# Two successive norms as one factor at the seam of two blocks, with X normed beside the next projection

## The chip, the cores and the metric

The kernel runs on one NeuronCore of a Trainium2 chip. The metric is the device time of one execution in microseconds. Engines are named as in the profile: PE is TensorE (matmuls), PEld its weight loads, DVE is VectorE, ACT is ScalarE, POOL is GpSimd, SP issues the weight DMAs.

## The reference

A token matrix X (256 tokens of 1024 features) passes through a first block of two layers, a final norm, and a second block of two layers. The parts at the seam:

```python
def _rmsnorm(x, g):
    x32 = x.astype(jnp.float32)
    y = x32 * lax.rsqrt(jnp.mean(x32 * x32, axis=-1, keepdims=True) + EPS)
    return (y * g.astype(jnp.float32)).astype(x.dtype)
...
    # the end of a layer of first_block
        gate = jax.nn.sigmoid((_rmsnorm(x, g[3]) @ ple_w_gate[li]).astype(jnp.float32))
        x = x + (gate * (p[li] @ ple_w_in[li]).astype(jnp.float32)).astype(x.dtype)
...
    return _rmsnorm(x, final_norm)
...
def second_block(x, c, w_ada, b_ada, g_pre, g_post, w_in, w_out, pe_k, pe_v, w_ck1, w_ck2, w_cv1, w_cv2):
    cs = jax.nn.silu(c)
    for l in range(DEPTH):
        mod = cs @ w_ada[l] + b_ada[l]
        shift, scale, gate = mod[:, None, :D], mod[:, None, D:2 * D], mod[:, None, 2 * D:]
        h = rmsnorm(x, g_pre[l]) * (1.0 + scale) + shift
        y = hybrid_mixer(h, w_in[l], w_out[l], pe_k[l], pe_v[l], w_ck1[l], w_ck2[l], w_cv1[l], w_cv2[l])
        x = x + gate * rmsnorm(y, g_post[l])
```

`hybrid_mixer` begins with `u = h @ w_in`. So the final norm of the first block is followed at once by the first norm of the second block. With r1 the first norm's factor of a token and G the final gain, the second factor is 1/sqrt(mean((x r1 G)^2) + EPS).

## The kernel before, in words

X lies in SBUF transposed: 128 partitions by 8 tiles (k) of 256 tokens; a "pair" m or j is two tiles, 512 columns. A sum over features is a matmul of `ones` with squares (`sums_pair`), which leaves the sum of each token in every partition of a PSUM bank.

Each engine runs its own program, written out by hand; engines wait for each other by semaphore counts (`when(name)` is the count at which the step `name` is done, `did(...)` counts a step). An engine works strictly in the order of its program, so whatever stands behind a waiting instruction waits too.

All weights stream through one ring of chunks of 1 MB. SP loads a chunk into one of two buffers `w_raw`, in two halves. `hi(c)` on ACT rounds it to `w_hi`, `lo(c)` on DVE makes the rest `w_lo`; both have four slots. A load of chunk c waits for `lo(c - 2)`, a `hi(c)` for PE's end of chunk c - 4. PE multiplies each chunk in three passes (`three`), which is 48 matmuls of 256 columns for a group of 256 output features. In the names below `ple1` has five chunks (c to c + 4) and the next, c + 5, is `win0`, the first of the 16 of the second block's projection; `AHEAD` is 3.

The work around the change, in program order:

- `ple(1, 9, 7, 7)`: the gate of layer 1. PE makes four groups into banks 4 to 7 (`pgate`). For each group j, DVE multiplies it by the norm factor `rs` into `pg`, ACT takes the sigmoid, and DVE's `finish(j)` multiplies by `pp` and adds to X. ACT squares each finished pair (`last_squares`): once plain into `sq`, and once with the final gain as scale into `sq_f`.
- PE sums both sets pair by pair, `sums_pair(8, m)` and `sums_pair(9, m, sq_f)`. Ahead of the last pair stands `mod_sums(3, 1)`: 24 one-column matmuls that sum the second block's modulation over partitions, into bank 1; `modulation` on DVE adds the bias into `mods`.
- The final norm: `root(8)` (Sqrt on ACT) and `inv(8)` (reciprocal on DVE) give r1. DVE multiplies the weighted sums by r1 squared (`mean_f`), ACT takes the Sqrt of that. POOL has multiplied X by G, and POOL and DVE multiply it by r1, two pairs each.
- The norm of layer l = 0 of the second block: `inv(9)`, then for each tile `scaled(k)` on DVE, `xh` on ACT (rounded, with the shift added) and `xl` on DVE (the rest).
- The projection, 16 groups of `WIN` (`qm`, `qm`, `km`, `km`, `vm`, ...) into banks 0 to 7 in turn. The first group takes the tiles as they come; DVE or ACT copies each group out (`proj`). While PE is on group n, ACT and DVE make `hi` and `lo` of chunk `win0` + n + 3.
- Ahead of its copies DVE builds the tables `bias` and `cbias`. X itself is next read at the end of the layer, where the mixer's output is added.

Of the kernel before, what the change touches and what calls it, by code (L numbers as in the profile page):

```python
# [24 lines left out]
P = 128  # L25
# [89 lines left out]
def chunk_table():  # L115
# [11 lines left out]
    return first, n  # L127


def build(nc, io, known):  # L130
# [396 lines left out]
    def _(pool):  # L527
        did = Steps(at)
        nc.gpsimd.memset(ones[:, :], 1.0).then_inc(*did(pool_steps))
        nc.gpsimd.memset(eps[:, :], EPS).then_inc(*did(pool_steps, "memsets"))  # L530
# [111 lines left out]
        for m in range(4):  # L642
            pool.wait_ge(*when(("sq", 9, m)))
            gain = col0[:, 95 + 2 * m:97 + 2 * m].unsqueeze(2).to_broadcast([P, 2, T])
            G.tensor_tensor(X[:, 2 * m:2 * m + 2, :], X[:, 2 * m:2 * m + 2, :], gain, ALU.mult).then_inc(*did(pool_steps, ("x_gain", m)))
        pool.wait_ge(*when(("rs", 8)))
        for m in (2, 3):
            pool.wait_ge(*when(("x_gain", m)))
            G.tensor_tensor(X[:, 2 * m:2 * m + 2, :], X[:, 2 * m:2 * m + 2, :], rep(rs[:, :], 2), ALU.mult).then_inc(*did(pool_steps, ("x", 9, m)))
        pool.wait_ge(*when(("sums", 9)))  # L650
        for l in range(2):

            pool.wait_ge(*when(("x", 9 + l, 3)))
# [3 lines left out]

            for kv, name in enumerate(("ck", "cv")):
# [10 lines left out]
    def _(act):  # L669
# [192 lines left out]
        def ple(l, nu, v, s):  # L862
            c = first[f"ple{l}"]
            norm(nu, v, g_norm(l, 3), s, ("chunk", first[f"out{2 * l + 1}"] - 1), [c - 1 + AHEAD, c + AHEAD])
            for j in range(4):
                if j in (0, 2):
                    hi(c + 1 + j + AHEAD)
                if j == 0:
                    hi(c + 2 + AHEAD)
                    root(s)  # L870
                if l == 0 and j >= 1:
                    high(5, 4, g_kv, j - 1, xh2)
                if l == 1 and j >= 1:
                    last_squares(j - 1)
                act.wait_ge(*when(("pg", l, j)))
                A(pg[:, 2 * j:2 * j + 2, :], pg[:, 2 * j:2 * j + 2, :], ACT.Sigmoid).then_inc(*did(act_steps, ("pgs", l, j)))
            if l == 0:
                high(5, 4, g_kv, 3, xh2)
            else:
                last_squares(3)  # L880
            hi(c + 4 + AHEAD)

        def last_squares(m):
# [3 lines left out]
            A(sq[:, pair_, :], X[:, pair_, :], ACT.Square).then_inc(*did(act_steps, ("sq", 8, m)))  # L887
            for k in (2 * m, 2 * m + 1):
                A(sq_f[:, k, :], X[:, k, :], ACT.Square, scale=g_final(k)).then_inc(*did(act_steps, ("sq", 9, m)))
# [98 lines left out]
        root(8)  # L988
        act.wait_ge(*when("mean_f"))
        A(std[:, :], std[:, :], ACT.Sqrt, bias=eps[:, :], scale=1.0 / D).then_inc(*did(act_steps, ("std", 9)))  # L990

        for l in range(2):
# [8 lines left out]
            c0 = first[f"win{l}"]  # L1001
# [1476 lines left out]
```

## Time and profile before

| what | value |
|---|---|
| device time, median of 3 runs | 1559.37 us (1559.15 to 1560.65) |
| the profiled execution: its time | 1557.95 us |
| the profiled execution: its span | 1556.1 us |
| mean granted clock of TensorE | 0.979 of full |
| PE busy | 1491.3 us, 96% of the span |
| DVE, ACT, POOL busy | 70%, 49%, 12% |

The span runs from the first to the last instruction of one profiled execution, and all times of rows are microseconds from its start. "Idle before <-releaser" tells how long an engine stood before an instruction and whose step it waited for. A granted clock of 1.00 is 2.4 GHz, 0.50 is 1.2 GHz.

### The profile page before, as it was taken

Reading aid. Unit: us, or ns where it says so; the run is one execution under the profiler, and the core shown is the slowest. Engines: PE = TensorE matmul, PEld = TensorE weight load, DVE = VectorE, ACT = ScalarE, POOL = GpSimd, SP = SyncE. Lnnn points to the kernel's source line nnn. Section 1 sums busy time; section 2 is a strip of 40 time slices with the busy share of each in tenths; the row PEclk is TensorE's granted clock in tenths of the full one; section 3 lists DMA queues with packets and bytes.
Section 4 is the critical chain, followed back from the end, with each engine's and each line's share of the span. In section 5 each row is a group of like instructions: output and inputs, shape, how many; then the busy total and the mean of one; then the engine's idle time right before and its main releaser. Section 6 shows DMA issues by size and latency. Waiting matters only on the chain.

```text
span 1556.1 us, 31034 instructions
## 1 busy us (share of the span) xinstructions
PE 1491.3 (96%) x12371; PEld 1436.0 (92%) x12371; DVE 1095.1 (70%) x1566; ACT 766.3 (49%) x1149; POOL 189.7 (12%) x227
## 2 busy tenths in 40 slices
PE   6999998999999999999999999999996999989998
PEld 6999998999999998999999899999996996879867
DVE  5886568986896677876677755887568557395683
ACT  5554355465554356444454454544354436354472
POOL 1111013711331010101010001110012000010000
PEclk9999999999999999999999999999997998999999
DMA  7787743345787646766646135776653751066400
GB/s 226 230 271 231 246 147 124 90 128 162 236 271 229 211 136 191 246 219 215 217 129 177 55 122 173 233 251 218 223 160 108 208 149 55 1 181 186 125 1 28
DMA packets 219308, 264.86 MB, mean 170 GB/s; under 512 B 22253, under 2 KB 197325, under 8 KB 219213
## 3 DMA queue, kind: packets, MB, share of 16 engines
q1 hardware_dynamic: 209136, 234.58, 48.5%
q0 software_dynamic: 8960, 27.37, 5.3%
q10 hardware_dynamic: 1117, 1.57, 0.3%
q8 instruction: 68, 1.11, 0.3%
q14 instruction: 27, 0.22, 0.1%
HBM read 262.44 MB, written 1.05 MB: 169 GB/s over the span
## 4 chain that ended last, share of the span: by engine, by line
PE 81%; DVE 12%; ACT 4%; DMA 2%; issue 1%; POOL 0%; SPq 0%; DVEq 0%; ACTq 0%
PE twin L1081 24%; PE twin L1082 24%; PE twin L1083 24%; DVE w_lo L1774 3%; DMA w_raw<-in_ffn_w_in 1%; PE twin L1488 1%; PE twin L1700 1%; ACT w_hi L700 1%; DVE rs L1803 1%; DVE hg_s L1992 1%; PE twin L1502 1%; PE twin L1500 1%; PE twin L1662 1%; DVE hg_f L1974 1%; DVE sq L1973 1%
## 5 line engine op out<-in xcount | busy, mean ns | idle before, releaser
L700 ACT ACTIVATE w_hi<-w_raw 128x1024 fp32r<-128x1024 f32 (+1 forms) x452 | 453.6, 1038 | 459.3 <-PE twin L1083 279.9
L1081 PE MATMUL twin<-xh,w_lo 128*128 128x256 f32 x2312 | 653.5, 283 | 26.2 <-DVE xl L2260 15.0
L1774 DVE TENSOR_TENSOR w_lo<-w_raw,w_hi 128x1024 fp32r<-128x1024 f32 (+1 forms) x452 | 548.1, 1249 | 166.0 <-ACT w_hi L700 165.6
L1082 PE MATMUL twin<-xl,w_hi 128*128 128x256 f32 x2312 | 648.4, 280 | 0.0
L1083 PE MATMUL twin<-xh,w_hi 128*128 128x256 f32 x2312 | 648.2, 280 | 0.0
L1081 PEld LDWEIGHTS twin<-xh,w_lo 128*128 128x128 f32 x2312 | 440.3, 190 | 31.4 <-DVE xl L2260 16.1
L1082 PEld LDWEIGHTS twin<-xl,w_hi 128*128 128x128 f32 x2312 | 439.6, 190 | 1.5 <-issue 1.2
L1083 PEld LDWEIGHTS twin<-xh,w_hi 128*128 128x128 f32 x2312 | 438.1, 189 | 0.2
L1081 PE MATMUL twin<-hh,w_lo 128*128 (+1 forms) x704 | 195.6, 278 | 0.0
L1082 PE MATMUL twin<-hl,w_hi 128*128 (+1 forms) x704 | 195.2, 277 | 0.0
L1083 PE MATMUL twin<-hh,w_hi 128*128 (+1 forms) x704 | 195.2, 277 | 0.0
L543 POOL DMA_DIRECT2D mod_raw<-in_w_ada x128 | 68.9, 542 | 527.4 <-DVE mod_acc L1823 401.2
L1081 PEld LDWEIGHTS twin<-hh,w_lo 128*128 128x128 f32 x704 | 132.9, 189 | 0.0
L1082 PEld LDWEIGHTS twin<-hl,w_hi 128*128 128x128 f32 x704 | 132.2, 188 | 0.0
L1083 PEld LDWEIGHTS twin<-hh,w_hi 128*128 128x128 f32 x704 | 132.1, 188 | 0.0
L1823 DVE SCALAR_TENSOR_TENSOR mod_acc<-mod_raw,csf,mod_acc 128x384 f32<-128x384 f32 x112 | 65.2, 617 | 39.7 <-DMA mod_raw<-in_w_ada 39.4
L622 POOL TENSOR_TENSOR sq<-sq 128x1024 f32<-128x1024 f32 x7 | 16.9, 2408 | 394.3 <-ACT sq L722 394.3
L706 ACT ACTIVATE xh<-X,col 128x256 fp32r<-128x256 f32 x72 | 32.0, 500 | 49.8 <-DVE X L1797 27.8
L665 POOL TENSOR_TENSOR y<-y,rs 128x512 f32<-128x512 f32 x4 | 6.9, 1738 | 343.5 <-DVE rs L1803 343.5
L1850 DVE TENSOR_TENSOR gate_t<-twin,rs 128x512 f32<-128x512 f32 x44 | 30.2, 687 | 26.1 <-PE twin L1083 26.0
L1858 DVE TENSOR_TENSOR up_t<-twin,rs 128x512 f32<-128x512 f32 x44 | 30.2, 686 | 23.6 <-PE twin L1083 23.6
L1081 PE MATMUL twin<-w_hi,xl 128*128 128x256 f32 x160 | 45.5, 285 | 0.0
(363 smaller groups left out, 2077.4 us busy)
## 6 DMA issues: line engine op xcount, KB each, us to landing
w_raw<-in_ffn_w_in SPq DMA_DIRECT2D x176, 512.0 KB, 4.7
w_raw<-in_ffn_w_out SPq DMA_DIRECT2D x88, 512.0 KB, 4.2
w_raw<-in_w_in SPq DMA_DIRECT2D x52, 512.0 KB, 4.7
mod_raw<-in_w_ada POOLq DMA_DIRECT2D x128, 192.0 KB, 4.4
w_raw<-in_a_w_in SPq DMA_DIRECT2D x32, 512.0 KB, 4.2
w_raw<-in_ple_w_gate SPq DMA_DIRECT2D x16, 512.0 KB, 4.2
w_raw<-in_b_w_out SPq DMA_DIRECT2D x16, 512.0 KB, 3.7
w_raw<-in_w_out SPq DMA_DIRECT2D x16, 512.0 KB, 4.5
```

Of the source, the lines that this page charges most:

```text
L543: pool.dma_start(mod_raw[:, n % 2, :], io["w_ada_2"][l][P * k:P * (k + 1), col:col + MOD_COLS]).then_inc(sem[f"mod_landed{n % 2}"], 16)
L622: G.tensor_tensor(sq[:, 0:4, :], sq[:, 0:4, :], sq[:, 4:8, :], ALU.add).then_inc(*did(pool_steps))
L700: A(w_hi[:, c % NSLOT, cols], w_raw[:, c % NRAW, cols], ACT.Copy).then_inc(*did(hi_ready))
L706: A(xh[:, k, :], X[:, k, :], ACT.Copy, scale=gain(k)).then_inc(*did(act_steps, ("xh", nu, k)))
L1081: mm(out, lhs[1], rhs[0], start=start, stop=False, skip_group_check=skip)
L1082: mm(out, lhs[0], rhs[1], start=False, stop=False, skip_group_check=skip)
L1083: return mm(out, lhs[0], rhs[0], start=False, stop=stop, skip_group_check=skip)
L1488: last = nc.tensor.transpose(bank[4 + h][:, dst * P:(dst + 1) * P], p[:, h, src * P:(src + 1) * P], ident)
L1774: V.tensor_tensor(w_lo[:, c % NSLOT, cols], w_raw[:, c % NRAW, cols], f32(w_hi[:, c % NSLOT, cols]), ALU.subtract).then_inc(*did(lo_ready))
L1823: V.scalar_tensor_tensor(acc, raw, cs, acc, ALU.mult, ALU.add).then_inc(sem["mod_steps"], 1)
L1850: V.tensor_tensor(gate_t[:, p % 2, :, :], two(bank[b][:, :]), rep(rs[:, :], 2), ALU.mult).then_inc(*did(gate_scaled))
L1858: V.tensor_tensor(up_t[:, p % 2, :, :], two(bank[b + 1][:, :]), rep(rs[:, :], 2), ALU.mult).then_inc(*did(up_scaled))
```

## The change

The final norm and the next norm become one factor. Since r1 = 1/sqrt(mean(x^2) + EPS), the product of both factors is 1/sqrt(mean((G^2 + EPS) x^2) + EPS^2). So one sum of squares, weighted by the root of G^2 + EPS (`gain_r`, computed once from the gains), gives the factor that takes X to the normed input of the projection; G itself goes into `gpre`. The plain squares are still summed, after the weighted ones; their factor (`std` 9 in the old tile `cos`, its reciprocal in `sin`) is made during the projection and applied to X there, one tile in each of the turns 4 to 11. POOL no longer multiplies X. In `ple(1)` DVE takes the products of groups 0 and 1 before `finish(0)` and so on, ACT takes each sigmoid before the squares of the pair before, and a Sqrt of one column stands before the last squares. `mod_sums(3, 1)` moves behind the third group of the projection, its `modulation` to DVE's fourth turn; POOL's loads of the compression weights (`wc`) wait for it. Two `lo` move behind `finish(3)` and behind the `xl`.

```diff
@@ POOL
-        for m in range(4):
-            pool.wait_ge(*when(("sq", 9, m)))
-            gain = col0[:, 95 + 2 * m:97 + 2 * m].unsqueeze(2).to_broadcast([P, 2, T])
-            G.tensor_tensor(X[:, 2 * m:2 * m + 2, :], X[:, 2 * m:2 * m + 2, :], gain, ALU.mult).then_inc(*did(pool_steps, ("x_gain", m)))
-        pool.wait_ge(*when(("rs", 8)))
-        for m in (2, 3):
-            pool.wait_ge(*when(("x_gain", m)))
-            G.tensor_tensor(X[:, 2 * m:2 * m + 2, :], X[:, 2 * m:2 * m + 2, :], rep(rs[:, :], 2), ALU.mult).then_inc(*did(pool_steps, ("x", 9, m)))
         pool.wait_ge(*when(("sums", 9)))
         for l in range(2):
-            pool.wait_ge(*when(("x", 9 + l, 3)))
+            pool.wait_ge(*when(("x", 8 + 2 * l, 3)))
...
+            pool.wait_ge(*when(("modsum", 3)))
             for kv, name in enumerate(("ck", "cv")):
...
@@ ACT, ple
                     root(s)
+                    if l == 1:
+                        act.wait_ge(*when("gain_c"))
+                        A(small[:, GAIN_C:GAIN_C + KD], small[:, GAIN_C:GAIN_C + KD], ACT.Sqrt).then_inc(*did(act_steps, "gain_r"))
                 if l == 0 and j >= 1:
                     high(5, 4, g_kv, j - 1, xh2)
+                act.wait_ge(*when(("pg", l, j)))
+                A(pg[:, 2 * j:2 * j + 2, :], pg[:, 2 * j:2 * j + 2, :], ACT.Sigmoid).then_inc(*did(act_steps, ("pgs", l, j)))
                 if l == 1 and j >= 1:
                     last_squares(j - 1)
-                act.wait_ge(*when(("pg", l, j)))
-                A(pg[:, 2 * j:2 * j + 2, :], pg[:, 2 * j:2 * j + 2, :], ACT.Sigmoid).then_inc(*did(act_steps, ("pgs", l, j)))
             if l == 0:
                 high(5, 4, g_kv, 3, xh2)
             else:
+                A(small[:, EPS2 - 1:EPS2], small[:, EPS2:EPS2 + 1], ACT.Sqrt).then_inc(*did(act_steps))
                 last_squares(3)
             hi(c + 4 + AHEAD)
@@ ACT, last_squares
             act.wait_ge(*when(("x", 8, m)))
-            A(sq[:, pair_, :], X[:, pair_, :], ACT.Square).then_inc(*did(act_steps, ("sq", 8, m)))
+            act.wait_ge(*when("gain_r"))
             for k in (2 * m, 2 * m + 1):
-                A(sq_f[:, k, :], X[:, k, :], ACT.Square, scale=g_final(k)).then_inc(*did(act_steps, ("sq", 9, m)))
+                A(sq[:, k, :], X[:, k, :], ACT.Square, scale=small[:, GAIN_C + k:GAIN_C + k + 1]).then_inc(*did(act_steps, ("sq", 8, m)))
+            A(sq_f[:, pair_, :], X[:, pair_, :], ACT.Square).then_inc(*did(act_steps, ("sq", 9, m)))
@@ ACT, after ple(1)
-        root(8)
-        act.wait_ge(*when("mean_f"))
-        A(std[:, :], std[:, :], ACT.Sqrt, bias=eps[:, :], scale=1.0 / D).then_inc(*did(act_steps, ("std", 9)))
+        act.wait_ge(*when(("sums", 8)))
+        act.wait_ge(*when(("rs", 7)))
+        A(std[:, :], bank[sums_bank(8)][:, 0:T], ACT.Sqrt, bias=small[:, EPS2:EPS2 + 1], scale=1.0 / D).then_inc(*did(act_steps, ("std", 8)))
@@ ACT, ahead of the projection's turns
+            if l == 0:
+                act.wait_ge(*when(("sums", 9)))
+                A(cos[:, :], bank[sums_bank(9)][:, 0:T], ACT.Sqrt, bias=eps[:, :], scale=1.0 / D).then_inc(*did(act_steps, ("std", 9)))
@@ PE
         for m in range(4):
-            if m == 3:
-                mod_sums(3, 1)
             sums_pair(8, m)
+        for m in range(4):
             sums_pair(9, m, sq_f)
-        release[sums_bank(9)] = "mean_f"
...
                 project(n, name, j)
+                if l == 0 and n == 2:
+                    mod_sums(3, 1)
@@ DVE, ple
+            def normed(j):
+                dve.wait_ge(*when(("pgate", l, j)))
+                V.tensor_tensor(pg[:, 2 * j:2 * j + 2, :], two(bank[4 + j][:, :]), rep(rs[:, :], 2), ALU.mult).then_inc(*did(dve_steps, ("pg", l, j)))
+
+            lo(c + 1 + AHEAD)
+            lo(c + 2 + AHEAD)
+            inv(s)
+            if l == 1:
+                normed(0)
+                normed(1)
+                finish(0)
+                normed(2)
+                finish(1)
+                finish(2)
+                normed(3)
+                finish(3)
+                lo(c + 3 + AHEAD)
+                return
...
@@ DVE, around ple(1)
+        V.tensor_tensor(small[:, GAIN_C:GAIN_C + KD], col0[:, 95:95 + KD], col0[:, 95:95 + KD], ALU.mult).then_inc(*did(dve_steps))
+        dve.wait_ge(*did.last)
+        V.tensor_scalar(small[:, GAIN_C:GAIN_C + KD], small[:, GAIN_C:GAIN_C + KD], EPS, None, ALU.add).then_inc(*did(dve_steps, "gain_c"))
         ple(1, 9, 7, 7)
-        inv(8)
-        V.tensor_tensor(std[:, :], rs[:, :], rs[:, :], ALU.mult).then_inc(*did(dve_steps))
-        dve.wait_ge(*did.last)
-        dve.wait_ge(*when(("sums", 9)))
-        V.tensor_tensor(std[:, :], std[:, :], bank[sums_bank(9)][:, 0:T], ALU.mult).then_inc(*did(dve_steps, "mean_f"))
-        for m in (0, 1):
-            dve.wait_ge(*when(("x_gain", m)))
-            V.tensor_tensor(X[:, 2 * m:2 * m + 2, :], X[:, 2 * m:2 * m + 2, :], rep(rs[:, :], 2), ALU.mult).then_inc(*did(dve_steps, ("x", 9, m)))
@@ DVE, the second block
             if l == 0:
-                dve.wait_ge(*when(("x", 9, 3)))
-            inv(s)
-            dve.wait_ge(*when(("sums", s)))
+                dve.wait_ge(*did.last)
+                V.tensor_tensor(gpre[:, :], gpre[:, :], col0[:, 95:95 + KD], ALU.mult).then_inc(*did(dve_steps))
+            inv(s if l else 8)
+            dve.wait_ge(*when(("sums", s if l else 8)))
...
             if l == 0:
-                modulation(3, 1)
+                lo(first["win0"] + 2)
...
             for n, (name, j) in enumerate(WIN[:15]):
                 lo(c0 + n + AHEAD)
+                if l == 0 and n == 3:
+                    modulation(3, 1)
+                    dve.wait_ge(*when(("std", 9)))
+                    V.reciprocal(sin[:, :], cos[:, :]).then_inc(*did(dve_steps, ("rs", 9)))
+                    dve.wait_ge(*did.last)
+                if l == 0 and 4 <= n < 4 + KD:
+                    V.scalar_tensor_tensor(X[:, n - 4, :], X[:, n - 4, :], g_final(n - 4), sin[:, :], ALU.mult, ALU.mult).then_inc(*did(dve_steps, ("x", 9, (n - 4) // 2)))
```

## Rows read from the trace of the kernel before

**Rows 1.** The page: busy time of each engine; the last chain by engine.

```profile
PE 1491.3 (96%) x12371; PEld 1436.0 (92%) x12371; DVE 1095.1 (70%) x1566; ACT 766.3 (49%) x1149; POOL 189.7 (12%) x227
...
PE 81%; DVE 12%; ACT 4%; DMA 2%; issue 1%; POOL 0%; SPq 0%; DVEq 0%; ACTq 0%
```

**Rows 2.** Windows at the seam: us, busy of engines (instructions), granted clock, DMA.

```profile
1180.00:1192.00 12.00, 1.15 (x4) 0.45 (x2) 11.39 (x15) 4.23 (x7) 7.35 (x10) 0.50 0.45 125
1192.00:1197.00 5.00, 5.00 (x24) 5.00 (x25) 4.97 (x15) 3.66 (x7) 0.13 (x1) 0.50 0.61 129
1197.00:1202.00 5.00, 5.00 (x46) 5.00 (x46) 5.00 (x19) 2.69 (x3) 0.00 (x0) 1.00 0.00 0
```

**Rows 3.** Timeline to the projection: start us, us, instruction, [idle before <-releaser].

```profile
1168.21 1.02 PE L1106 MATMUL twin<-sq,ones 128*128 128x256 f32 x4
...
1176.61 0.69 DVE L2082 TENSOR_TENSOR X<-X,pg 128x512 f32<-128x512 f32 x1
1177.34 0.63 ACT L887 ACTIVATE sq<-X 128x512 f32<-128x512 f32 x1 [1.91 <-DVE X L2082]
...
1178.67 1.99 ACT L700 ACTIVATE w_hi<-w_raw 128x1024 fp32r<-128x1024 f32 x2
...
1180.68 1.28 ACT L730 ACT_TABLE_LOAD   x1
1181.97 0.47 ACT L730 ACTIVATE std<-twin,eps 128x256 f32<-128x256 f32 x1
1182.48 1.75 DVE L1803 RECIPROCAL rs<-std 128x256 f32<-128x256 f32 x1 [0.37 <-ACT std L730]
...
1188.32 1.75 DVE L1803 RECIPROCAL rs<-std 128x256 f32<-128x256 f32 x1
...
1191.92 0.55 PE L1081 MATMUL twin<-xh,w_lo 128*128 128x256 f32 x1 [10.85 <-DVE xl L2260]
...
1195.26 1.27 DVE L2260 SCALAR_TENSOR_TENSOR xl<-sq,mods,xh 128x256 fp32r<-128x256 f32 x3
```

**Rows 4.** Timeline of the gate turns of layer 1, ACT and DVE.

```profile
1161.80 0.69 DVE L2093 TENSOR_TENSOR pg<-twin,rs 128x512 f32<-128x512 f32 x1
...
1162.53 0.63 ACT L876 ACTIVATE pg<-pg 128x512 f32<-128x512 f32 x1 [1.25 <-DVE pg L2093]
...
1163.92 0.69 DVE L2082 TENSOR_TENSOR X<-X,pg 128x512 f32<-128x512 f32 x1
...
1164.53 0.68 DVE L2093 TENSOR_TENSOR pg<-twin,rs 128x512 f32<-128x512 f32 x1
...
1164.64 0.64 ACT L887 ACTIVATE sq<-X 128x512 f32<-128x512 f32 x1 [1.48 <-DVE X L2082]
...
1166.50 1.99 ACT L700 ACTIVATE w_hi<-w_raw 128x1024 fp32r<-128x1024 f32 x2
...
1168.39 2.35 DVE L1774 TENSOR_TENSOR w_lo<-w_raw,w_hi 128x1024 fp32r<-128x1024 f32 x2
```

**Rows 5.** Timeline of DVE beside the projection.

```profile
1196.64 0.42 DVE L2272 SCALAR_TENSOR_TENSOR bias<-const 128x256 bf16<-128x256 f32 x1
...
1200.15 1.20 DVE L1774 TENSOR_TENSOR w_lo<-w_raw,w_hi 128x1024 fp32r<-128x1024 f32 x1
...
1210.91 0.69 DVE L2289 COPY km<-twin 128x512 f32<-128x512 f32 x1 [0.54 <-PE twin L1083]
...
1216.35 0.69 DVE L2289 COPY km<-twin 128x512 f32<-128x512 f32 x1 [1.93 <-PE twin L1083]
```

**Rows 6.** Timeline of PE: one of four `mod_sums` bursts.

```profile
800.83 2.73 PE L1153 MATMUL twin<-ones,mod_acc 128*128 128x1 f32 x24
```

**Rows 7.** Windows: a stretch behind that burst, columns as in rows 2.

```profile
804.60:807.80 3.20, 3.20 (x17) 3.16 (x15) 3.06 (x3) 0.00 (x0) 0.00 (x0) 0.50 0.53 170
```

**Rows 8.** DMA issues from 1150 to 1200: KB each, median us to landing.

```profile
w_raw<-in_w_in SPq DMA_DIRECT2D x10, 512.0 KB, 4.7
...
wc<-in_w_ck POOLq DMA_DIRECT2D x1, 512.0 KB, 5.3
```

More of the change, by code:

```diff
@@ L127, in chunk_table @@
     return first, n
+EPS2, GAIN_C = 52, 53
 def build(nc, io, known):
@@ L529, in _ @@
         nc.gpsimd.memset(ones[:, :], 1.0).then_inc(*did(pool_steps))
+        nc.gpsimd.memset(small[:, EPS2:EPS2 + 1], EPS * EPS).then_inc(*did(pool_steps))
         nc.gpsimd.memset(eps[:, :], EPS).then_inc(*did(pool_steps, "memsets"))
@@ L2082, in finish @@
                 V.tensor_tensor(X[:, pair_, :], X[:, pair_, :], pg[:, pair_, :], ALU.add).then_inc(*did(dve_steps, ("x", v + 1, j)))
+            def normed(j):
[15 more added lines that the diff above has]
+                return
             for j in range(4):
-                if j in (0, 2):
+                if j == 2:
                     lo(c + 1 + j + AHEAD)
-                if j == 0:
-                    lo(c + 2 + AHEAD)
-                    inv(s)
-                dve.wait_ge(*when(("pgate", l, j)))
-                if l == 0 and j == 2:
                     modulation(1)
-                V.tensor_tensor(pg[:, 2 * j:2 * j + 2, :], two(bank[4 + j][:, :]), rep(rs[:, :], 2), ALU.mult).then_inc(*did(dve_steps, ("pg", l, j)))
-                if l == 0 and j >= 1:
+                normed(j)
+                if j >= 1:
                     low(5, g_kv, j - 1, xh2, xl2)
                 finish(j)
-            if l == 0:
-                low(5, g_kv, 3, xh2, xl2)
+            low(5, g_kv, 3, xh2, xl2)
             lo(c + 4 + AHEAD)
@@ L2247, in _ @@
             if l == 0:
-                dve.wait_ge(*when(("x", 9, 3)))
-            inv(s)
-            dve.wait_ge(*when(("sums", s)))
+                dve.wait_ge(*did.last)
+                V.tensor_tensor(gpre[:, :], gpre[:, :], col0[:, 95:95 + KD], ALU.mult).then_inc(*did(dve_steps))
+            inv(s if l else 8)
+            dve.wait_ge(*when(("sums", s if l else 8)))
             def scaled(k):
```

## The prediction

> **What bounds the kernel now.** I read the page first. TensorE (PE) is busy for 96% of the span, and the chain that ended last runs on PE for 81% of it and on VectorE (DVE) for 12% [rows 1]. So a microsecond counts only where PE stands still or where PE itself gets less to do. The seam that the change edits is such a place: PE is busy for 1.15 of the 12 us from 1180 to 1192, its granted clock there is 0.50, and it stays at 0.50 until 1197, in which time it starts 24 matmuls where the next 5 us hold 46 [rows 2]. Work on ScalarE (ACT) or DVE matters here only if it stands in the chain that ends with PE's first projection matmul at 1191.92, which had idled 10.85 us for its operand `xl` [rows 3]. I then followed that chain backward in the timeline. The last quarter of X is done at 1177.30 (1176.61 and 0.69). Squares follow on ACT, then two `w_hi` halves, a table load, a Sqrt, a reciprocal that ends at 1184.23, the final norm of X, and a second reciprocal that ends at 1190.07 [rows 3]. All of it lies on the path; PE's sums between them are short (1.02 for a pair of tiles [rows 3]).
>
> The sum is made on the axis of the profiled execution, 1557.95 us with a span of 1556.1. The median of the three runs is 1559.37, 1.4 more; I take the difference from the profile and subtract it from the median.
>
> **Gate turns (layer 1).** Before, the second sigmoid sits behind the first pair's squares on ACT, and DVE's next product behind `finish`. Durations: product with `rs` 0.69, sigmoid 0.63, each of the two ops in `finish` 0.69, back-to-back start 0.61 after the one before on DVE [rows 4]; the three squares of one pair hold ACT for 1.33 (1177.34 to 1178.67) and two `w_hi` halves for 1.99 [rows 3]. The new order, on the old axis: product 0 at 1161.80 as before, product 1 at 1162.41 to 1163.10, sigmoid 0 at 1162.53, sigmoid 1 right behind it to 1163.77, X of pair 0 at 1164.61 as before. ACT squares pair 0 from 1164.64 to 1165.98, then stands in the `w_hi` halves of `win0`+1 until 1167.9, as it does now from 1166.50 without a wait [rows 4]. So sigmoid 2 is at 1167.9 to 1168.5 although product 2 was done at 1165.2; that turn is bound by ACT. `finish(2)` ends at 1169.95 and product 3 at 1170.55; sigmoid 3 follows to 1171.21, `finish(3)` to 1172.65. X is whole 4.65 us earlier than 1177.30. POOL's multiplications of X by the final gain go away; POOL is on no link of the chain, so that is 0. What moves behind `finish(3)` is the `w_lo` of `win0`+1 (two halves, 2.35 [rows 4]); PE wants that only at its second projection, so the 12 us from its new end, about 1175, to that projection cover it.
>
> **One norm in place of two.** From the first reciprocal's end (1184.23) to the second's (1190.07) lie 5.84 us [rows 3]: two small DVE products, a Sqrt, the multiplication of X, `gpre` and `gpost`, a reciprocal. All leave the path. One Sqrt and one reciprocal stay. The chain after X is whole is then: ACT ends pair 2's squares at 1172.5 and takes the dummy Sqrt, whose table load is 1.28 and moves ahead of the squares [rows 3]; the one-column Sqrt behind it is bounded by 0 and by the 256-wide one's 0.47 [rows 3], and I take 0.2, near the middle. Squares of pair 3 from 1174.0, both halves done at 1174.9; the unweighted square and the `w_hi` halves of `win0`+2 keep ACT until 1177.3. PE needs 1.0 (2.0 at half clock) for the last weighted sums, so it is done at 1176 to 1177, under those halves. Sqrt to 1177.75, reciprocal (1.75) to 1179.55. From reciprocal to first matmul it was 1.85 (1190.07 to 1191.92), so PE can start at 1181.4 instead of 1191.92, 10.5 earlier. The small ops (`gain_c`, its Sqrt after `root(7)`, one more `gpre` product, a memset at the start) run while their engines wait: 0. Bound of this part: 9.5 to 11.5, an ACT wait of a microsecond either way.
>
> The table load has a page. The row shows 1.28, starting 0.02 after the preceding op's end and followed at once by its Sqrt [rows 3]. The Trainium skill, ScalarE: Activation LUTs, section "What ACT_TABLE_LOAD costs", adds a drain of about 1.38 us to each switch, 2.66 in all. By the page's figure the start would be an estimated 1.4 us later and the time about 1552.7; no such drain stands in these rows, and I follow them.
>
> **Sums of the unweighted squares.** All four pairs now run after the weighted ones, in front of the projection in PE's queue: 4 x 1.02 = 4.1 us at full clock [rows 3], 8.2 at half. They cover the wait for the norm if they end by 1181.4. PE has three short bursts in the 6.7 us before 1175, less than it had before the fall at 1180, so I expect the clock to fall here already and to come back after about 5 us of unbroken work, as from 1192 to 1197 [rows 2]: about 1180. That gives 1.5 us of the sums between 1177.0 and 1180, the other 2.6 at full speed, end at 1182.6. The projection then starts at full clock. Its operands come over 4.6 us (`xl` ends at 1196.53, 4.6 after PE's start [rows 3]), so the first group ends between 1187.4 (start 1181.4, operands) and 1188.0 (start 1182.6, 5.44 of work): I take 1187.7. Before, groups end 5.44 apart, the third with the copy at 1210.91 [rows 5], so the first ended at 1200.0. Gain so far 12.3: 10.5 of earlier start and 1.8 of clock.
>
> **`mod_sums(3)` inside the projection.** Before, its 24 one-column matmuls stood in a stretch where PE waited anyway. Now they stand between the third and fourth groups, where PE waits for nothing: 2.7 us (2.73 for the 24 [rows 6]). And the clock: behind the burst at 800.83 the granted clock is 0.50 from 804.6 to 807.8, 17 matmuls in 3.2 us, with PE busy throughout [rows 7]. The same stands behind the bursts at 248 and 569 (three in all), and the fall at 1180 follows the fourth. A half-clock stretch gives 24 for 46 [rows 2], so 3.2 us of it lose 1.5. Bounds: 0 if no fall, 1.5; I take 1.5, since all four have it.
>
> The rule that speaks the other way: the Trainium skill, TensorE: Matmul & The Clock Gate, section "HAM oscillation — how this bites in real kernels", puts the fall down to idle gaps of PE between groups of matmuls. By it a burst with PE busy on both sides would cost its 2.7 alone; these rows disagree.
>
> **X in the projection.** A reciprocal (1.75), one small add and eight 256-wide products join DVE between copies, where it idles 1.93 in a turn of 5.44 [rows 5]. A product is under the 0.69 of a 512-wide copy, so one a turn fits, and the reciprocal comes when three chunks are ahead. It waits there for `mod_sums(3)` with the copy of the fourth group queued behind it, whose bank PE takes again eight groups later. ACT's Sqrt for it waits for the unweighted sums, which end ahead of the projection, and holds back only the `w_hi` of `win0`+3, wanted three groups later. POOL's four `wc` loads wait for `mod_sums(3)` and land in 5.3 [rows 8], long before PE wants them; beside the weight stream they could delay one chunk by that much, under the two groups (10.9) that it is ahead. Cost 0 while that cover stands.
>
> **Sum.** 12.3 - 2.7 - 1.5 = 8.1. Time 1559.4 - 8.1 = 1551.3 (0.52% less; about 0.2%, 3.1 us, is what a measurement of this kernel can tell from no change).
>
> **Rivals.**
> (a) No clock fall behind `mod_sums(3)`, because PE is busy ahead of it, in it and behind it: 12.3 - 2.7 = 9.6, 1549.8. Against it stand four bursts of four. The clock gate's page, above, would have it so.
> (b) The clock stays low through the sums: they end at 1185.2, the first group takes the 8.1 that it took before (1191.92 to 1200.0) and ends at 1193.3; 6.7 - 2.7 - 1.5 = 2.5, 1556.9. For it: it stayed low for 17 us before, to 1197. Against it: most of those had no work, and the sums are unbroken work.
> (c) The weights absorb it: `win0`+4 is loaded only after `w_lo` of `win0`+2, which moves behind the `xl`. Landing 4.7 [rows 8] after about 1188.4, its `w_lo` is done at 1197.2, and PE wants it at about 1206.7. Slack 9.5; a load of over twice the usual would eat the gain: about 1559.
> (d) Slower: before `mod_sums(3)` PE takes bank 1, and so waits for DVE's copy of the second group. On DVE that copy now stands behind the last `xl` (1186.0), `win0`+2 (2.35), the bias block (3.5, from 1196.64 to 1200.15 [rows 5]), `win0`+3, the first copy, `win0`+4: 1197.9, while PE comes at 1187.7 + 10.9 = 1198.6. Slack is 0.7, and each microsecond beyond costs one. It becomes no gain at 8.1 of waiting and slower by over 0.2% at 11.2: 1562.5 or more. A microsecond or two of it is likely enough and lies in the range.
>
> **How the numbers follow.** Forecast 0.72, (a) 0.13, (b) 0.06, (c) 0.05, (d) 0.04. Faster: the forecast, (a) and a third of (b), 0.87. Same: the rest of (b) and (c), 0.09. Slower: (d), 0.04. The range 1548.3 to 1555.5 holds the forecast with its bounds (9.5 to 11.5 of start, a bank wait of up to 2, the half-clock stretch of 0 to 1.5) and (a) whole.
>
> **What would show it.** X whole near 1172.7 and the table load ahead of the last squares; one Sqrt and one reciprocal between; the first projection matmul at 1181 to 1183 with the granted clock near 1.0 by then; first group's end near 1187.7; a gap of 2.7 between third and fourth group, with a half-clock stretch behind it; the `km` copy of the fourth group at about 1208 instead of 1216.35 [rows 5]; from there a constant offset of some 8 us to the end. I would be wrong if the clock is still 0.50 when the projection runs, or if PE waits for bank 1 ahead of the burst.

## The result, and the profile after

| | before | after |
|---|---|---|
| device time, median of 14 runs each | 1552.86 us (1547.03 to 1562.98) | 1545.06 us (1536.75 to 1552.45) |
| ratio, with its 95% interval | | 0.9947 (0.9922 to 0.9971) |
| the profiled execution: its span | 1556.1 us | 1534.9 us |

The change makes the kernel 0.53% faster; 0.0053 of 1552.86 is 8.2 us, and the interval of the ratio reaches from 4.5 to 12.1 us. The forecast was 8.1 us less, and 1551.3 as a time. So the difference came out and the time did not: the 14 runs of before have a median 6.5 us under the 1559.37 that I subtracted from.

The page of the changed kernel, as in [rows 1]:

```profile
PE 1479.2 (96%) x12371; PEld 1423.3 (93%) x12371; DVE 1093.6 (71%) x1573; ACT 766.7 (50%) x1151; POOL 181.7 (12%) x222
...
PE 77%; DVE 13%; ACT 5%; DMA 3%; issue 1%; POOL 0%; SPq 0%; DVEq 0%; ACTq 0%
```

PE has the same number of instructions and 12.1 us less busy time, so what it lost is time per instruction (a higher clock, or the pace that is shown below under before_again), not work.

The seam, timeline of the changed kernel (start us, us, instruction, idle before and its releaser), the rows that answer to [rows 3, 4]. Its first product with `rs` is at 1152.80, 9.00 earlier than before [rows 4], so 9.00 added to a time here puts it on the axis of the prediction.

```profile
1152.80 1.29 DVE L2091 TENSOR_TENSOR pg<-twin,rs 128x512 f32<-128x512 f32 x2
1153.53 1.23 ACT L874 ACTIVATE pg<-pg 128x512 f32<-128x512 f32 x2 [1.15 <-DVE pg L2091]
...
1156.98 2.00 ACT L697 ACTIVATE w_hi<-w_raw 128x1024 fp32r<-128x1024 f32 x2
...
1158.88 0.62 ACT L874 ACTIVATE pg<-pg 128x512 f32<-128x512 f32 x1
...
1162.96 0.69 DVE L2087 TENSOR_TENSOR X<-X,pg 128x512 f32<-128x512 f32 x1
...
1163.54 1.28 ACT L880 ACT_TABLE_LOAD   x1
...
1164.94 0.89 ACT L890 ACTIVATE sq<-X,small 128x256 f32<-128x256 f32 x2
...
1165.89 2.07 PE L1111 MATMUL twin<-sq,ones 128*128 128x256 f32 x4 [0.78 <-ACT sq L890]
...
1166.26 1.99 ACT L697 ACTIVATE w_hi<-w_raw 128x1024 fp32r<-128x1024 f32 x2
1167.76 4.70 PE L1111 MATMUL twin<-sq_f,ones 128*128 128x256 f32 x16
1168.16 0.45 ACT L992 ACTIVATE std<-twin,small 128x256 f32<-128x256 f32 x1
1168.64 1.75 DVE L1808 RECIPROCAL rs<-std 128x256 f32<-128x256 f32 x1 [2.36 <-ACT std L992]
...
1172.25 0.36 PE L1086 MATMUL twin<-xh,w_lo 128*128 128x256 f32 x1
...
1189.16 2.73 PE L1158 MATMUL twin<-ones,mod_acc 128*128 128x1 f32 x24
...
1191.76 0.36 PE L1086 MATMUL twin<-xh,w_lo 128*128 128x256 f32 x1
...
1197.76 0.69 DVE L2307 COPY km<-twin 128x512 f32<-128x512 f32 x1 [0.97 <-PE twin L1088]
```

X is whole at 1163.65, which is 1172.65 on the old axis (forecast 1172.65). The table load stands ahead of the last squares, and its one-column Sqrt starts 0.02 us behind it (1164.84). One Sqrt and one reciprocal of 256 columns are left on the path. The first projection matmul is at 1181.25 on the old axis (forecast 1181.4), and PE has no idle time before it: the 16 matmuls that sum the unweighted squares, 4.70 us, fill PE until the operands are there. The burst takes 2.73 between the third and fourth groups. The copy of the fourth group is at 1206.76 (forecast about 1208).

Windows of the same stretch (us, busy of PE, PEld, DVE, ACT, POOL, granted clock, DMA share, GB/s), answering to [rows 2]:

```profile
1157.40:1163.10 5.70, 3.58 (x23) 2.67 (x21) 2.95 (x6) 4.93 (x10) 0.00 (x0) 1.00 0.00 0
1163.20:1169.80 6.60, 5.82 (x13) 4.20 (x14) 4.21 (x7) 5.38 (x9) 0.00 (x0) 0.50 0.53 156
1169.95:1172.40 2.45, 2.45 (x13) 2.05 (x12) 2.42 (x6) 1.30 (x3) 0.00 (x0) 1.00 0.01 2
1172.40:1178.00 5.60, 5.60 (x47) 5.50 (x47) 5.60 (x14) 4.34 (x8) 0.32 (x3) 1.00 0.02 3
1189.00:1192.10 3.10, 3.10 (x30) 3.10 (x30) 2.49 (x3) 2.14 (x3) 0.00 (x0) 1.00 0.97 319
1192.10:1197.00 4.90, 4.90 (x44) 4.90 (x43) 4.66 (x5) 1.35 (x2) 3.97 (x5) 1.00 0.91 266
```

The granted clock is 0.50 while PE has only the short sums, and 1.00 again before the projection starts; PE had nothing but its queue of sums in between. Behind the burst it does not fall in this execution: 44 matmuls in 4.9 us.

From the first product to the copy of the fourth group it was 54.55 before (1161.80 [rows 4] to 1216.35 [rows 5]) and is 44.96 now: 9.6 less, which is 12.3 - 2.7 as in rival (a). But the two profiled spans differ by 21.2. Of that, 9.0 lies ahead of the first product, in layers that the change does not touch, and 2.6 behind the copy of the fourth group. This was the first sign that single executions differ by more than the change is worth.

### The profile page after: what moved, and what is told of

The parts are those of the page before. It is cut to its first block, busy times and chain, and to the rows that moved or that the text cites. A ratio compares the mean times of both kernels' runs of the same rounds, so it can differ in the third digit from the quotient of the medians.

```text
span 1534.9 us, 31039 instructions
## 1 busy us (share of the span) xinstructions
PE 1479.2 (96%) x12371; PEld 1423.3 (93%) x12371; DVE 1093.6 (71%) x1573; ACT 766.7 (50%) x1151; POOL 181.7 (12%) x222
## 3 DMA queue, kind: packets, MB, share of 16 engines
q8 instruction: 68, 1.11, 0.3%
## 4 chain that ended last, share of the span: by engine, by line
PE 77%; DVE 13%; ACT 5%; DMA 3%; issue 1%; POOL 0%; SPq 0%; DVEq 0%; ACTq 0%
PE twin L1086 23%; PE twin L1087 23%; PE twin L1088 23%; DVE w_lo L1779 4%; DMA w_raw<-in_ffn_w_in 2%; PE twin L1493 1%; ACT w_hi L697 1%; PE twin L1703 1%; PE twin L1111 1%; DVE rs L1808 1%; DVE hg_s L1997 1%; PE twin L1507 1%; PE twin L1505 1%; DVE hg_f L1979 1%; DVE sq L1978 1%
## 5 line engine op out<-in xcount | busy, mean ns | idle before, releaser
L1087 PE MATMUL twin<-w_lo,xh 128*128 128x256 f32 x160 | 45.2, 283 | 0.0
L1088 PE MATMUL twin<-w_hi,xh 128*128 128x256 f32 x160 | 45.1, 282 | 0.0
```

Source lines behind the costliest of these rows:

```text
L1087: mm(out, lhs[0], rhs[1], start=False, stop=False, skip_group_check=skip)
L1088: return mm(out, lhs[0], rhs[0], start=False, stop=stop, skip_group_check=skip)
```

## Experiments

Since the times scatter, the edits were read at the seam. All times in this table are us, read from one profiled execution of each kernel, from the layer's first product with `rs` to the start of what the column names (X: to the end of its last quarter). G1 and G4 are the last matmul of the first and fourth projection groups; km4 is the start of the copy of the fourth. The last column is the ratio to before with its interval, where more than one execution was timed. before_again, after_again and after_third are the two kernels unchanged.

| kernel | X whole | Sqrt | first matmul | burst | G1 | G4 | km4 | ratio |
|---|---|---|---|---|---|---|---|---|
| before | 15.50 | 20.17 | 30.12 | 14.19 | 37.91 | 54.23 | 54.55 | |
| after | 10.85 | 15.36 | 19.45 | 36.37 | 25.37 | 44.58 | 44.96 | 0.9947 |
| mod_back | 10.86 | 15.36 | 19.72 | 11.23 | 25.42 | 42.38 | 44.09 | 0.9934 (0.9897 to 0.9971) |
| old_turns | 14.66 | 17.92 | 22.16 | 39.42 | 27.99 | 47.43 | 47.82 | 0.9946 (0.9909 to 0.9983) |
| new_turns | 10.86 | 15.56 | 26.64 | 11.82 | 33.57 | 50.53 | 50.85 | 0.9976 (0.9946 to 1.0005) |
| best1 | 9.14 | 12.69 | 18.80 | 12.34 | 25.54 | 42.50 | 45.44 | 0.9925 (0.9898 to 0.9953) |
| best2 | 9.15 | 12.70 | 18.27 | 12.35 | 24.51 | 40.83 | 43.20 | 0.9887 (0.9852 to 0.9921) |
| best3 | 9.91 | 14.57 | 18.68 | 7.77 | 24.58 | 40.90 | 44.46 | 0.9906 (0.9870 to 0.9941) |
| burst_twice | 10.85 | 15.35 | 20.12 | 36.65 | 25.66 | 52.20 | 52.58 | |
| before_again | 15.51 | 20.18 | 30.13 | 14.20 | 37.52 | 53.84 | 54.15 | |
| after_again | 10.86 | 15.35 | 19.45 | 36.86 | 25.43 | 45.07 | 45.46 | |
| after_third | 10.86 | 15.36 | 19.45 | 36.85 | 25.43 | 46.58 | 46.97 | |

The intervals of the ratios are 0.25 to 0.37% wide to each side, 4 to 6 us, so none of them separates two kernels whose seams differ by 2 us. In mod_back and best1 to best3 km4 tells of DVE and not of PE: there DVE is busy with the reciprocal `sin` (1.75) or ahead of it when the fourth group ends, and copies the group only behind it. PE does not stand still for that copy in any of the four, so G1 and G4 are compared there instead.

**mod_back** is after with the burst put where PE waits, ahead of the last weighted sums, and its `modulation` ahead of the projection on DVE.

```diff
         for m in range(4):
+            if m == 3:
+                mod_sums(3, 1)
             sums_pair(8, m)
...
-                if l == 0 and n == 2:
-                    mod_sums(3, 1)
...
+                modulation(3, 1)
```

> The changed kernel with the mod_sums burst back ahead of the last weighted sums, and its modulation behind the xl. The seam is measured from layer 1's first product with rs to the copy of the fourth group: 54.55 us before, 44.96 in the changed kernel. Theory (the burst costs its 2.7 us where PE waits for nothing, and 0 to 1.5 of clock behind it; ahead of the last sums it hides under the two w_hi halves that ACT makes there): seam 42.2, time 2.7 to 4.2 us under the changed kernel, ratio to the kernel before near 0.992. Rival (the old place is on the path too, since PE's last weighted sums come later by what the burst takes and the Sqrt waits for them): seam 43 to 45, ratio as the changed kernel's 0.995.

The seam of 44.09 is what the rival forecast, but not for its reason: the Sqrt does not wait (15.36 in both), and G1 is where it was (25.42 and 25.37). The burst is hidden in the wait for the last squares; what is late is only DVE's copy, behind the reciprocal (1203.91 and 1.75, copy at 1205.69). Three groups later PE is 2.2 ahead of after, though its groups took 5.65 there against after's 5.44; at equal pace (see before_again) it would be 2.8. So the burst inside the projection costs its own length and saves nothing. The ratio alone (0.9934 beside 0.9947) could not have told this.

**old_turns** is after with the gate turns of before.

```diff
+                if l == 1 and j >= 1:
+                    last_squares(j - 1)
                 act.wait_ge(*when(("pg", l, j)))
...
-                normed(0)
-                normed(1)
-                finish(0)
...
+                for j in range(4):
+                    if j == 2:
+                        lo(c + 3 + AHEAD)
+                    normed(j)
+                    finish(j)
```

> The changed kernel with layer 1's gate turns in their old order on DVE and ACT. Theory (turns are worth 4.65 us, added to the norm's 5.85): X is whole 15.5 after the first product as before, seam 49.6, ratio to the kernel before about 0.997 to 0.998. Rival (the turns hide behind the one-column Sqrt's table load, or the norm alone gives the whole gain): seam under 46.5.

X is whole 3.8 later than in after, the Sqrt only 2.6 and the first matmul 2.7 later; km4 is 2.9 later. The seam lies between the theory's 49.6 and the rival's 46.5: the turns are worth less here than the 4.65 that X gains. The reason is in ACT's order: with the new turns DVE is done first, and the third pair's squares and the table load (1163.54, 1.28) stand between X and its last squares. With the old turns that load ran from 1171.75 to 1173.03, ended before X was whole at 1173.18, and cost nothing. The forecast had this ACT wait in its sum.

X is also whole 0.84 earlier than in before, with the same order of turns. Timeline of before, beside the same `finish` in old_turns:

```profile
1166.15 1.05 POOL L645 TENSOR_TENSOR X<-X,col 128x512 f32<-128x512 f32 x1 [17.31 <-ACT sq_f L889]
...
1166.63 1.11 DVE L2080 TENSOR_TENSOR pg<-pg,pp 128x512 f32<-128x512 f32 x1 [1.42 <-ACT pg L876]
```

```profile
1163.35 0.69 DVE L2085 TENSOR_TENSOR pg<-pg,pp 128x512 f32<-128x512 f32 x1 [1.42 <-ACT pg L876]
```

In before DVE's product of `pg` and `pp`, both in SBUF, starts while POOL multiplies X by the gain, and takes 1.11 instead of 0.69; the last turn has the same (1.12 beside POOL's 1.04). Twice 0.42 is the 0.84. So with the old turns POOL was on the path after all, through DVE. The product with `rs` in between, which reads a PSUM bank, is not slowed (0.68 at 1170.66, inside POOL's 1.63 from 1170.01).

**new_turns** is before with the new gate turns alone; both `lo` stand behind the last `finish`.

```diff
+                act.wait_ge(*when(("pg", l, j)))
...
                 if l == 1 and j >= 1:
                     last_squares(j - 1)
-                act.wait_ge(*when(("pg", l, j)))
...
+                normed(0)
+                normed(1)
+                finish(0)
+                normed(2)
+                finish(1)
+                finish(2)
+                normed(3)
+                finish(3)
+                lo(c + 3 + AHEAD)
+                lo(c + 4 + AHEAD)
```

> The kernel before with the new order of layer 1's gate turns alone, both w_lo that stood between them put behind the last finish. Theory: X is whole 10.85 after the first product instead of 15.5, and the rest of the chain is as before, so the seam is 54.55 - 4.65 = 49.9, ratio about 0.997. Rival (the two w_lo, 4.7 us on DVE, now stand between the last finish and the reciprocal and give the gain back): seam 52 to 55, ratio 1.000.

X is whole at the same place as in after, though POOL still multiplies it by the gain, the first matmul is 3.5 earlier than in before and km4 3.7 earlier. The ratio's interval (0.9946 to 1.0005) does not tell this kernel from before; the seam does. Of the 4.65 that X gains 1.2 is lost on DVE, where four `w_lo` halves now stand ahead of the reciprocal:

```profile
1166.64 6.31 DVE L1774 TENSOR_TENSOR w_lo<-w_raw,w_hi 128x1024 fp32r<-128x1024 f32 x4
1173.05 1.75 DVE L1803 RECIPROCAL rs<-std 128x256 f32<-128x256 f32 x1
```

At the first matmul the two parts alone give 3.5 and, in old_turns, 8.0; together, in after, they give 10.7. The 0.8 between is near POOL's 0.84, which either part alone takes off the path. That this is the reason is not shown, since new_turns and after each have another wait of about a microsecond (here the 1.2 on DVE, there the table load). At G1 the parts overlap by 1.7 (4.3 and 9.9 against 12.5), for either part alone already saves some of the half-clock stretch.

**best1** tries to take out ACT's waits: two `w_hi` halves move into its gaps, half of the unweighted sums go between the weighted ones, and the burst stands behind the last weighted sums.

```diff
+                if l == 1 and j == 3:
+                    hi(c + 3 + AHEAD, None, [0])
...
                 last_squares(3)
+                hi(c + 3 + AHEAD, None, [1])
...
             sums_pair(8, m)
-        for m in range(4):
+            if m < 2:
+                sums_pair(9, m, sq_f)
+        mod_sums(3, 1)
+        for m in (2, 3):
             sums_pair(9, m, sq_f)
```

> The changed kernel with three further moves: the w_hi halves of win0+1 behind the second squares and behind the last squares, those of win0+2 behind the Sqrt; the unweighted sums of pairs 0 and 1 in PE's gaps between the weighted ones; the mod_sums burst behind the last weighted sums. Theory (ACT's w_hi halves bind the third turn and the Sqrt): X whole 9.3 after the first product instead of 10.85, first projection matmul 17.2 after it instead of 19.45, seam 40 (2.4 of ACT and 2.7 of the burst under the changed kernel), ratio 0.991. Rival (PE's queue of sums and burst is then the bound ahead of the projection, and the clock falls behind the burst): first matmul 18.5 or later and a half-clock start, seam 42 to 43.

ACT's part came out: the Sqrt is 2.7 earlier than in after. The projection did not follow: its first matmul is at 18.80, where the rival had it, and G1 is not earlier at all (25.54). PE's timeline in best1 shows why:

```profile
1169.31 1.13 PE L1116 MATMUL twin<-sq,ones 128*128 128x256 f32 x4 [0.76 <-ACT sq L894]
1170.27 3.40 PE L1163 MATMUL twin<-ones,mod_acc 128*128 128x1 f32 x24
1173.53 3.76 PE L1116 MATMUL twin<-sq_f,ones 128*128 128x256 f32 x8
```

The clock fell inside the burst (3.40 instead of 2.73), the eight sums behind it took 3.76, and the clock came back only at 21.05, behind the start of the projection. PE's own queue had become the bound. In after, too, the 16 sums last until the first projection matmul and the first `xl` starts at 1171.62; the norm's chain and PE's queue end there within half a microsecond.

**best2** shortens that queue: POOL adds the four pairs of unweighted squares into one, and PE sums two tiles instead of eight. The diff is against best1.

```diff
+        for m in range(1, 4):
+            pool.wait_ge(*when(("sq", 9, m)))
...
+            G.tensor_tensor(sq_f[:, 0:2, :], sq_f[:, 0:2, :], sq_f[:, 2 * m:2 * m + 2, :], ALU.add).then_inc(*did(pool_steps, ("folded", 9)))
...
             sums_pair(8, m)
-            if m < 2:
-                sums_pair(9, m, sq_f)
         mod_sums(3, 1)
-        for m in (2, 3):
-            sums_pair(9, m, sq_f)
...
+        for k in range(2):
+            last = mm(bank[sums_bank(9)][:, 0:T], ones[:, :], sq_f[:, k, :], start=(k == 0), stop=(k == 1))
```

> The first faster try with the unweighted squares folded by POOL from eight tiles to two before PE sums them, so that PE's queue ahead of the projection is the weighted sums (4.1), the burst (2.6 to 3.1) and 1.0 to 2.0 more, and not 4.1 more. Theory (in the first try PE's queue of sums and burst, done 18.7 after the first product, kept the projection from starting at 16.9): first matmul at 16.9 to 17.5, first group's last matmul near 23.5 instead of 25.5, ratio near 0.991. Rival (POOL's additions slow DVE's finish beside them, or the clock is at half when the projection starts): first group's end 25 or later.

G1 is 0.9 earlier than in after and 1.0 earlier than in best1, less than was hoped, since the burst now took 4.57 of PE's time at half clock:

```profile
1170.27 4.57 PE L1168 MATMUL twin<-ones,mod_acc 128*128 128x1 f32 x24
1174.70 2.05 PE L1583 MATMUL twin<-sq_f,ones 128*128 128x256 f32 x4
```

With the burst out of the projection G4 is 3.8 earlier than in after. The ratio of best2 is the lowest of all, 0.9887 from six runs; the interval just clears that of after. Taken as they stand the ratios differ by 0.6%, the seam's 3.8 us are 0.24%, so part of that is scatter. Both readings support that best2 beats both kernels; by how much it beats after is not settled.

**best3** puts the burst behind the first weighted sums, where the clock is still full, and six matmuls that nothing reads behind the sums. The diff is against best2.

```diff
             sums_pair(8, m)
-        mod_sums(3, 1)
+            if m == 0:
+                mod_sums(3, 1)
...
+        keep_clock(6)
```

> The second faster try with the mod_sums burst behind the first weighted sums, while the clock is still full, and six matmuls that keep PE busy (into a bank that nothing reads) ahead of the projection. Theory (the burst took 4.4 us there because it ran at half clock; behind the first sums it takes 2.6, and the Sqrt waits 0.5 more for the last sums): first matmul of the projection 17.4 to 18.0 after layer 1's first product instead of 18.3, first group's last matmul 23.4 to 24.0 instead of 24.5, ratio to the kernel before 0.988 to 0.990. Rival (the clock falls sooner behind a burst that stands there, and the projection starts at half clock): first group's end 25 or later.

The burst took 2.73 there and the clock was back at 15.13, sooner than in any other kernel. But it had fallen at 11.72, the last weighted sums ran at half clock and the Sqrt came at 14.57 instead of 12.70, so G1 stayed (24.58), between the theory's 24.0 and the rival's 25. Not all of the 1.9 is the burst's: 0.8 of it is X, whole later than in best2 because DVE waited 0.86 for PE's fourth gate group. In best1 to best3 the half-clock stretch comes at another place each time, and each place costs another link.

**before_again, after_again, after_third** are both kernels unchanged, profiled again.

> The kernel before, unchanged. Theory (the base of the prediction is what moved: PE comes back from each half-clock stretch at one of two paces, 0.113 or 0.118 us per matmul at granted clock 1.00, and keeps it for a whole stage, so single times of one kernel lie over 1% apart): the span less what the slow pace costs is 1536, as in the first profile (1556.1 with 20.0 of it), within 3; the seam to the end of the first group is 37.9 from the first product; stages at the slow pace are others than in the first profile. Rival (1559 is the kernel's time and lower ones are another chip's): the same stages are slow as before.

> The changed kernel, unchanged. Theory: the seam is that of its first profile, first group's last matmul 25.4 after the first product, the burst at 36.3 with 2.6 for itself, clock behind it as it falls (1.00 in the first profile); span less slow pace 1524 within 3. Rival (the profile had luck in the seam): first group's end 27 or later.

> The changed kernel, unchanged, a third profile. Theory (whether the clock falls behind the burst is decided anew in each execution, near one in two): seam as before to the burst (first group's end 25.4, burst 2.6 for itself); the clock behind it falls or not, so the fourth group ends 44.6 to 45.1, or 1.6 later. Rival (in the projection it never falls): clock 1.00 again. The time is near 1545 within 10, as the pace has it.

The seams repeat: km4 at 54.15 in before_again (54.55), at 45.46 in after_again and 46.97 in after_third (44.96). Averaged over the profiles, 54.35 and 45.80: 8.6 less. The spans repeat less well: 1552.0 for before_again (1556.1), 1540.4 and 1546.4 for the two of after (1534.9). Windows of 80 us in the feed-forward parts, of before, before_again and after_third in this order:

```profile
400.00:480.00 80.00, 80.00 (x708) 80.00 (x708) 73.14 (x86) 42.73 (x49) 26.62 (x34) 1.00 0.81 259
640.00:720.00 80.00, 80.00 (x682) 80.00 (x681) 59.28 (x72) 35.67 (x43) 7.47 (x14) 1.00 0.72 227
```

```profile
400.00:480.00 80.00, 80.00 (x682) 80.00 (x681) 69.39 (x82) 39.72 (x46) 26.36 (x33) 1.00 0.76 246
640.00:720.00 80.00, 80.00 (x709) 80.00 (x708) 64.35 (x78) 39.90 (x47) 8.54 (x16) 1.00 0.76 245
```

```profile
400.00:480.00 80.00, 80.00 (x681) 80.00 (x680) 69.84 (x82) 39.82 (x46) 26.07 (x32) 1.00 0.78 251
640.00:720.00 80.00, 80.00 (x681) 80.00 (x681) 61.14 (x74) 36.89 (x44) 8.37 (x16) 1.00 0.73 233
```

PE is busy throughout and the granted clock is 1.00 in all six. Still PE starts 708 matmuls in one and 682 in another: 0.113 us each, or 0.117. The same stretch of the same kernel has either pace, and one execution changes between them. Added up over an execution (each spacing of two matmuls between 0.1155 and 0.121 us, less the 0.1133 of the faster pace), the slower pace costs 20.0 us in before, 15.3 in before_again, 11.1 in after, 19.8 in after_again and 25.6 in after_third. So 8.9 of the 12.1 us by which PE's busy time differs between the two pages is pace, and not the change. Without it the spans are 1536.1 and 1536.8 for before, and 1523.8, 1520.5 and 1520.9 for after: two kernels apart, though after_again misses the 1524 within 3 that was expected of it. They stand 14.7 apart on average, against 8.6 at the seam. Counted in the same way between the same matmuls, 4.4 of the other 6 stand between 200 and 350 us of the span, in layers that the change does not touch; there the three profiles of after differ from one another by 6.0 and the two of before by 4.0. So that is scatter too, and what makes it is not shown.

**burst_twice** is after with the burst of one-column matmuls issued twice in the projection; the extra 24 write columns that nothing reads.

```diff
+        if f == 3:
+            for n in range(2 * MOD):
+                mm(bank[b][:, 64 + n:65 + n], mod_acc[:, n * P:(n + 1) * P], ones[:, 0:1], start=True, stop=True)
```

> The changed kernel with the mod_sums burst issued twice in the projection, the first into columns of the bank that nothing reads. Theory (a burst of one-column matmuls is too little work for the clock, though PE is busy; one burst may slip through, two can't): 2.6 more for itself and a half-clock stretch behind it that costs 1.6, so the fourth group ends 48.3 to 49 after the first product instead of 44.6. Rival (the clock falls for idle gaps of PE alone, as the clock gate's page has it): 2.6 more and clock 1.00 throughout, 47.2.

G4 is 7.6 later than in after (52.20, behind the theory's 49 as well), not 2.7. Timeline and windows of burst_twice:

```profile
1205.13 2.73 PE L1159 MATMUL twin<-ones,mod_acc 128*128 128x1 f32 x24
...
1207.72 5.25 PE L1161 MATMUL twin<-ones,mod_acc 128*128 128x1 f32 x24
```

```profile
1204.50:1207.70 3.20, 3.20 (x31) 3.20 (x31) 2.18 (x2) 1.17 (x3) 0.00 (x0) 1.00 1.01 322
1207.90:1218.00 10.10, 10.10 (x48) 10.10 (x49) 4.95 (x6) 1.91 (x2) 3.97 (x5) 0.50 0.92 269
```

PE waits for nothing here, yet the clock is at 0.50 when the second burst starts and stays so for 10 us. At that clock the same 24 instructions take 5.25. The rest is the half-clock stretch over the fourth group. This is one execution: it shows that the clock can fall with no gap of PE ahead of it, not that two bursts always bring it down. The single burst gives the same fall at times; windows of after_third around its burst and behind:

```profile
1197.50:1200.60 3.10, 3.10 (x30) 3.10 (x29) 2.46 (x3) 1.55 (x2) 0.00 (x0) 1.00 1.03 334
1200.80:1204.00 3.20, 3.20 (x17) 3.20 (x17) 2.67 (x4) 1.42 (x2) 3.20 (x4) 0.51 1.01 307
1204.20:1208.00 3.80, 3.80 (x34) 3.80 (x33) 1.61 (x2) 0.29 (x1) 0.42 (x1) 0.99 1.05 281
```

Here 17 matmuls start in 3.2 us, as in [rows 7], and the fourth group takes 7.24 against 5.73 in after: 1.5, the forecast's term. It came in one of the four profiles with a single burst in the projection (not in after, after_again, old_turns).

## Why the prediction was right in its difference and wrong in its time

- **The base: the step that failed.** "The median of the three runs is 1559.37, 1.4 more; I take the difference from the profile and subtract it from the median." The three runs agreed within 0.1% and I took that for the kernel's scatter. Fourteen runs of before, these three among them, lie between 1547.03 and 1562.98 with a median of 1552.86, and 57 others between 1543.8 and 1567.2. The three were all from the upper part. Of the 57 only 10 lie over 1559, so three such values within 0.1% are hardly three independent draws; what they had in common is not shown. The pace is one source of the scatter (20.0 us of the profile that I took the axis from), but the three runs themselves left no trace. With the larger median the same sum gives 1552.86 - 8.1 = 1544.8, beside 1545.06 measured. The view that could have shown it was the window: [rows 5] have groups 5.44 apart, but a window elsewhere in the same trace holds 682 matmuls instead of 708 at a clock of 1.00, and I did not ask what the absolute time rests on. The 0.2% that I gave as what a measurement can tell was too fine as well: with 14 runs of each kernel the interval is 0.25% to each side.
- **The difference: right, and so near in part by luck.** The interval allows 4.5 to 12.1. With the terms as the profiles gave them (12.5, 2.7, and 0.4 for the fall on average, below) the sum would be 9.4; the seams, averaged, differ by 8.6.
- **Start of the projection: right.** 10.5 forecast; 30.12 - 19.45 = 10.7 measured. X whole, table load, squares and Sqrt came within 0.2 of their places, and new_turns and old_turns show that each of the two parts gains alone.
- **POOL "on no link of the chain": wrong, without harm.** Its multiplications cost DVE 0.84 in before. The 4.65 for the turns already held it, since I costed every product of the new order at 0.69; under the old order the removal alone is worth 0.84, under the new one nothing (X whole at 10.86 in new_turns).
- **First group: right.** 12.3 of gain forecast, 37.91 - 25.37 = 12.5 measured. The clock fell during the sums and was back ahead of the projection, as forecast; the sums were over by the first matmul's start, 1181.25 on the old axis, where 1182.6 was forecast. Rival (b) is out in all three profiles of after: the first matmul is at 19.45 in each.
- **The burst at 2.7: right.** 2.73 in the trace, and mod_back gets back 2.8 at equal pace. It is the dearest step of the change.
- **The fall behind the burst at 1.5, "since all four have it": right size, wrong certainty.** It came in one of four profiles with a single burst there, so on average it is 0.4; the forecast case and rival (a) were both seen. Behind the bursts near 569 and 800 it is not regular either: over the twelve traces it came 8 times behind the one and 5 times behind the other. One execution was too few, and two of its four bursts were another case: PE had idled 1.99 some 6 us ahead of the one at 248 and 2.34 some 2 us ahead of the fourth, while ahead of those at 569 and 800 it had not. The Trainium skill, TensorE: Matmul & The Clock Gate, section "HAM oscillation — how this bites in real kernels", puts such falls down to idle gaps; burst_twice, with PE busy ahead of, in and behind the bursts, shows one without a gap, and the measurement decides.
- **Rivals (c) and (d): not seen.** In after, the copy of the second group on DVE (1187.80 and 0.69) is done 0.67 before the burst starts, which is the slack of 0.7 that (d) gave, and PE does not stand still between the first projection matmul and the fourth group or in the 60 us behind it, so no weights are late.
- **What stays open.** What sets PE's pace at a full granted clock. Some changes of pace fall on the end of a half-clock stretch (in before at 603, in after at 576), others come with none near; no experiment was made on it. Nor is it shown what the three runs of the base shared.

## What to carry to other kernels

Take the base from as many runs as show the scatter: three that agree within 0.1% were all 0.4 to 0.5% above the median, which was nearly as much as the change is worth. A sum from the trace gives a difference well, and then the place to measure an edit of a few microseconds is the stretch around it, from one fixed instruction to another in each trace, not the total. Put small odd work (a burst of one-column matmuls) where the bounding engine waits anyway; inside its dense work it costs its full length and at times the clock behind it (here 2.7, and 1.5 in one profile of four).

## What the runs showed of the hardware that was not expected

- At a granted clock of 1.00 PE runs the same dense 256-column matmuls 0.113 or 0.117 us apart, for long stretches, and which it is differs between executions of one kernel; 11 to 27 us of a span of some 1550 over the twelve traces.
- The granted clock can fall to 0.50 behind or inside a burst of 24 one-column matmuls while PE never waits (8 of 12 traces behind the burst near 569, the doubled burst in the projection), and at 0.50 the burst takes 5.25 us instead of 2.73.
- A 128x512 product of two SBUF tiles on DVE takes 1.11 us instead of 0.69 when it starts while POOL multiplies another tile (one that reads PSUM stays at 0.68), and in best2 a 128x8 operation on DVE (`gpre`) takes 1.23 us instead of 0.16 beside POOL's additions.
